# A decoder step on one Trainium2 core: the last pass of two projections taken token tile by token tile

## The chip, the core and the metric

The kernel runs on one core of one Trainium2 chip. It is timed in device microseconds from launch to end, without profiling. Its engines are TensorE (PE: matmuls and transposes), VectorE (DVE), ScalarE (ACT), GpSimd (POOL) and SyncE (SP), which only issues DMAs here. Each engine runs its own list of instructions in order, and the lists wait for each other by semaphores that are written by hand.

## The reference, cut to what matters

One layer over 512 prompt tokens and 64 sample tokens (8 requests of 8), model width D = 1024, all in float32:

```python
def rms_norm(x, g):
    y = x32 * lax.rsqrt(jnp.mean(x32 * x32, axis=-1, keepdims=True) + EPS)
    return (y * g.astype(jnp.float32)).astype(x.dtype)
...
    h = rms_norm(x, ln1_pre_l) * (1 + sc1) + sh1
    mixed, new_state = mix_fn(h @ w_in_l)          # pooling heads and sparse attention
    x = x + g1 * rms_norm(mixed @ w_out_l, ln1_post_l)
    h = rms_norm(x, ln2_pre_l) * (1 + sc2) + sh2
    f = jnp.square(jax.nn.relu(h @ w_ff1_l)) @ w_ff2_l        # 1024 -> 4096 -> 1024
    x = x + g2 * rms_norm(f, ln2_post_l)
```

A norm over a row needs the sum of squares of all 1024 columns, so nothing of a token's output can be scaled before its last column is there.

## The kernel before, in words

**Token tiles.** Tokens lie on partitions: four prompt tiles of 128 (t = 0 to 3) and one tile with the 64 sample tokens (t = NT = 4), whose high and low parts are stacked on 128 partitions and added later. A projection's output of 512 columns is one PSUM bank, and tile t uses bank 3 + t, both for columns 0 to 511 (nh = 0) and for 512 to 1023 (nh = 1).

**Split weights.** Each float32 matmul is three matmuls of a high and a low part (two for the sample tile). A piece of weights (1 MB) is loaded by SP into `raw`, ACT writes its high part to `w_split` (L1168), DVE the low part (L486), and the semaphore `lo_ready` releases it to PE. `raw` and `w_split` have two slots each. The order of pieces is the list `PIECES`: `wo` 0 to 3 are the output projection (two halves of the contraction for nh = 0, then two for nh = 1), `w1` and `w2` the MLP in four quarters.

**Projections.** `by_token` (L948) takes one column half: the first piece over all tiles (0, 1, 2, 3, NT), then the second piece over all tiles; each tile's bank is full only in the second. ACT copies a full bank to `out_t`; for the sample tile ACT copies the low rows to `half_s` and DVE adds them (`sum_rows`, L1844; in the MLP L1907 and L1908).

**Between the two projections (called the middle below).** For each tile after nh = 1: ACT squares 1024 columns with a running sum (L1204), DVE turns the sum into a mean (L1558), ACT takes the root, DVE the reciprocal (L1565), DVE multiplies by it and the gate (`gated`, L1834), POOL adds the residual in `x_res` (L697), then square, mean, root and reciprocal again and DVE scales to `out_t` (`normalise`, L1570), two tiles behind (LAG = 2). PE then transposes (`turned_hidden`, L740): it waits until all five tiles are normalised (L779). ACT and DVE scale, shift and split the transposed rows while PE goes on, and the first MLP matmul follows.

**The end.** In the last quarter of the MLP with nh = 1 DVE adds each bank to `out_t` (L1897) as it gets full, and one tile behind does `last_residual` (L1837): gate, then residual (L1841). POOL stores 1024 columns of each tile (L705, L707), waits for the stores, and the program ends for all engines together (the trace puts the engines' last instructions on L269).

Of the kernel before, what the change touches and what calls it, by code (L numbers as in the profile page):

```python
# [21 lines left out]
D = 1024  # L22
# [23 lines left out]
LAG = 2  # L46
EARLY = 4
QF = 4
# [105 lines left out]
def plan_norms():  # L154


    order = [(0, t) for t in range(NT + 1)]
    for j in range(NT + 1 + LAG):
        order += [(1, j)] * (j <= NT) + [(2, j - LAG)] * (j >= LAG)
    order += [(3, t) for t in range(NT + 1)]  # L160
    return {key: n for n, key in enumerate(order)}


NORM = plan_norms()
# [102 lines left out]
def build_program(nc, a, o, spans):  # L267
    ctx = ExitStack()
    with ctx:  # L269
# [24 lines left out]
        ss = sb("ss", [128, 4 * (NT + 1)])  # L294
        rstd = sb("rstd", [128, 4 * (NT + 1)])
# [85 lines left out]
        halves_mlp = sb("halves_mlp", [128, 512], stack=mlp)  # L381
        mlp.close()
# [113 lines left out]
        def _(sp):  # L496
# [79 lines left out]
            for n in range(AT[("wo", 0)] + 2, len(PIECES)):  # L576
                load_piece(n)

        @block.gpsimd
        def _(pool):  # L580
# [121 lines left out]
            for t in range(NT + 1):  # L702
                pool.wait_ge(S["y_ok"], t + 1)
                if t < NT:
                    pool.dma_start(yp[:, t, :], x_res[:, t, :]).then_inc(S["y_out"], 16)  # L705
                else:
                    pool.dma_start(o["y_s"].rearrange("b t d -> (b t) d"), x_res[0:TS, t, :]).then_inc(S["y_out"], 16)  # L707
            pool.wait_ge(S["y_out"], 16 * (NT + 1))
# [6 lines left out]
        def _(pe):  # L715
# [431 lines left out]
            for nh in range(2):  # L1147
                by_token("wo", 2 * nh, ("wo", nh), act_hi, act_lo, act_s)
# [4 lines left out]
            for f in range(QF):  # L1153
# [4 lines left out]
                for nh in range(2):  # L1158
                    by_token("w2", 4 * f + 2 * nh, ("w2", f, nh), hid_hi, hid_lo, hid_s, f)
# [22 lines left out]
        def _(act):  # L1182
# [14 lines left out]
            def square(k, t, src):  # L1197

                r = rows_of(t)
                if NORM[k, t]:  # L1200
                    act.wait_ge(S["squares"], NORM[k, t])
                junk = stage[:, :, :].rearrange("p a n -> p (a n)")
                x = (NT + 1) * k + t
                run(junk[0:r, :], src[0:r, t, :], ACT.Square, accum_out=ss[0:r, x:x + 1]).then_inc(S["squares"], 1)  # L1204

            def root(k, t):
                x = (NT + 1) * k + t
                act.wait_ge(S["mean_ok"], NORM[k, t] + 1)
                run(rstd[0:rows_of(t), x:x + 1], ss[0:rows_of(t), x:x + 1], ACT.Sqrt).then_inc(S["root_ok"], 1)
# [17 lines left out]
            act.wait_ge(S["pad_zero2"], 1)  # L1227
            out = full(act, "cT")
# [12 lines left out]
            for t in range(NT + 1):  # L1241
                square(0, t, x_in)
# [233 lines left out]
            keep_tokens("wo", (), 0, True, 0, AT[("wo", 1)])  # L1476
            hi_until(AT[("wo", 2)] + 3)

            for j in range(NT + 1 + LAG):
                if j < NT:  # L1480
                    free(run(out_t[:, j, 512:D], full(act, ("wo", 1, j))[:, :]), ("wo", 1, j))
                elif j == NT:
                    out = full(act, ("wo", 1, NT))
                    evacuated(act, ("wo", 0, NT))
                    run(half_s[:, :], out[TS:2 * TS, :]).then_inc(S["low_rows"], 1)
                if j <= NT:
                    evacuated(act, ("wo", 1, j))
                    square(1, j, out_t)
                if j >= LAG:
                    act.wait_ge(S["residual"], j - LAG + 1)  # L1490
                    square(2, j - LAG, x_res)
                if j <= NT:
                    root(1, j)
                if j >= LAG:
                    root(2, j - LAG)
# [29 lines left out]
            for t in range(NT):  # L1525
                evacuated(act, ("w2", QF - 1, 1, t))
                square(3, t, out_t)
                root(3, t)
            keep_tokens("w2", (QF - 1,), 1, False, 1 + 2 * QF, 0)
            evacuated(act, ("w2", QF - 1, 1, NT))  # L1530
            square(3, NT, out_t)
            root(3, NT)

        @block.vector
        def _(dve):
# [18 lines left out]

            def mean(k, t):
                x, r = (NT + 1) * k + t, rows_of(t)
                dve.wait_ge(S["squares"], NORM[k, t] + 1)
                nc.vector.tensor_scalar(ss[0:r, x:x + 1], ss[0:r, x:x + 1], 1.0 / D, EPS, ALU.mult, ALU.add)\  # L1558
                    .then_inc(S["mean_ok"], 1)
# [379 lines left out]
```

## Time and profile before

| | us |
|---|---|
| median of three runs | 976.88 (974.75 to 990.48) |
| profiled execution, its own time | 972.49 |
| its span, first to last instruction | 970.8 |
| PE busy in the span | 861.6 (89%) |
| last matmul of the output projection to the first transpose | 488.9 to 509.0 |
| first to last matmul of the MLP | 517.6 to 949.9 |

The span is 1.69 us shorter than the time of the same execution. All times of the trace count from the start of the span. Each line of the page's parts names the source line, the engine, the operation, and output and inputs by the program's names; `bank` is PSUM.

### The profile page before, as it was taken

The page shows a single profiled execution, that of the slowest core. Times are in us where ns is not written, and L with a number is a line of the kernel's source. Part 1 is how long each engine was busy: PE and PEld are TensorE (multiplying, and loading weights), DVE is VectorE, ACT ScalarE, POOL GpSimd, SP SyncE. Part 2 cuts the span into 40 slices and gives each one's busy share as a digit, 9 for nine tenths or more (in the row PEclk, how much of TensorE's full clock was granted, in tenths as well). Part 3 has the DMA queues.
Part 4 walks back from the last instruction along what each step waited for, and adds up shares of the span by engine and source line. Part 5 has one row for each costly group of instructions (what it writes and reads, how often), then busy time and mean ns, then how long its engine had stood idle before and what let it go on. Part 6 is the DMA issues. An engine that isn't in the chain of part 4 may idle for free.

```text
span 970.8 us, 11293 instructions
## 1 busy us (share of the span) xinstructions
PE 861.6 (89%) x4136; PEld 646.7 (67%) x4136; DVE 453.4 (47%) x859; ACT 335.3 (35%) x615; POOL 97.9 (10%) x145
## 2 busy tenths in 40 slices
PE   2798899999978968879919999999999999999991
PEld 0486448877735545438816888888888888888880
DVE  0342899768466962311385441134334333343335
ACT  3453632242454742211447242233212331233121
POOL 2141210007032310000040000000000000000000
PEclk9889799999978997999969999999999999999996
DMA  9741300412385766654201212222122222222102
GB/s 327 261 126 51 95 11 2 129 52 66 122 271 185 246 211 202 195 174 163 86 22 44 87 54 77 87 87 87 59 72 87 87 87 70 67 82 86 44 1 98
DMA packets 68122, 105.83 MB, mean 109 GB/s; under 512 B 6906, under 2 KB 32134, under 8 KB 68058
## 3 DMA queue, kind: packets, MB, share of 16 engines
q1 hardware_dynamic: 62882, 94.12, 30.3%
q0 software_dynamic: 3952, 8.75, 2.7%
q10 hardware_dynamic: 1232, 2.23, 0.6%
q8 instruction: 33, 0.54, 0.2%
q14 instruction: 23, 0.19, 0.1%
HBM read 100.04 MB, written 5.15 MB: 108 GB/s over the span
## 4 chain that ended last, share of the span: by engine, by line
PE 70%; DVE 8%; issue 4%; ACT 3%; SPq 2%; DMA 1%; POOL 1%; ACTq 0%; DVEq 0%; POOLq 0%
PE bank L737 68%; PE bank L740 3%; DVE out_t L1834 1%; DVE score L1645 1%; ACT stage L1193 1%; DVE probs L1740 1%; SPq L535 1%; DVE keys L1547 1%; SPq L553 1%; ACT probs L1193 1%; DVE out_t L1570 1%; DMA raw<-in_ada_w 1%; DVE act_lo L1547 1%; DVE x_res L1841 1%; DMA pages<-in_cache_k 0%
## 5 line engine op out<-in xcount | busy, mean ns | idle before, releaser
L737 PE MATMUL bank<-act_hi,w_split 128*128 128x512 f32 (+1 forms) x800 | 259.9, 398 | 0.0
L486 DVE TENSOR_TENSOR w_split<-raw,w_split 128x2048 fp32r<-128x2048 f32 (+2 forms) x48 | 107.3, 2238 | 155.7 <-ACT w_split L1168 155.6
L737 PEld LDWEIGHTS bank<-act_hi,w_split 128*128 128x128 f32 (+1 forms) x800 | 151.7, 190 | 33.8 <-issue 1.0
L737 PE MATMUL bank<-w_split,hid_hi 128*128 128x512 f32 x512 | 161.2, 396 | 0.0
L737 PE MATMUL bank<-act_lo,w_split 128*128 128x512 f32 (+1 forms) x400 | 157.6, 394 | 0.0
L1168 ACT ACTIVATE w_split<-raw 128x2048 fp32r<-128x2048 f32 (+2 forms) x48 | 89.3, 1862 | 106.4 <-PE bank L737 106.4
L737 PEld LDWEIGHTS bank<-w_split,hid_hi 128*128 128x128 f32 x512 | 95.9, 188 | 22.9
L737 PE MATMUL bank<-w_split,hid_lo 128*128 128x512 f32 x256 | 101.3, 396 | 0.0
L737 PEld LDWEIGHTS bank<-act_lo,w_split 128*128 128x128 f32 (+1 forms) x400 | 76.0, 190 | 15.9
L737 PE MATMUL bank<-w_split,act_s 128*128 128x512 f32 (+1 forms) x248 | 60.6, 386 | 0.0
L737 PE MATMUL bank<-w_split,act_hi 128*128 128x512 f32 x192 | 59.6, 392 | 0.0
L737 PEld LDWEIGHTS bank<-w_split,hid_lo 128*128 128x128 f32 x256 | 48.1, 188 | 11.6
L1193 ACT ACTIVATE stage<-bank 128x512 f32<-128x512 f32 (+3 forms) x43 | 25.3, 587 | 83.9 <-PE bank L737 80.9
L1874 DVE TENSOR_TENSOR stage<-stage 128x512 f32<-128x512 f32 x32 | 22.2, 693 | 67.8 <-ACT stage L1193 66.2
L737 PEld LDWEIGHTS bank<-w_split,act_s 128*128 128x128 f32 x248 | 46.1, 188 | 9.4
L705 POOL DMA_DIRECT2D out_y_p<-x_res x4 | 2.1, 538 | 447.8 <-DVE x_res L1841 447.8
L737 PEld LDWEIGHTS bank<-w_split,act_hi 128*128 128x128 f32 x192 | 35.7, 188 | 8.0 <-issue 0.8
L737 PE MATMUL bank<-w_split,act_lo 128*128 128x512 f32 x96 | 37.4, 390 | 0.0
L1897 DVE TENSOR_TENSOR out_t<-bank,out_t 128x512 f32<-128x512 f32 x24 | 16.5, 689 | 36.1 <-PE bank L737 36.1
L737 PE MATMUL bank<-raw,c_pad 128*32 128x512 f32 x160 | 28.5, 794 | 5.0 <-DMA raw<-in_ada_w 5.0
L740 PE MATMUL bank<-cst,pages 128*128 128x128 f32 (+2 forms) x168 | 26.0, 303 | 7.6 <-DMA pages<-in_cache_k 5.8
L737 PE MATMUL bank<-w_split,hid_s 128*128 128x512 f32 x128 | 32.5, 396 | 0.0
(240 smaller groups left out, 1120.0 us busy)
## 6 DMA issues: line engine op xcount, KB each, us to landing
raw<-in_w_ff SPq DMA_DIRECT2D x32, 1024.0 KB, 5.3
raw<-in_ada_w SPq DMA_DIRECT2D x20, 1024.0 KB, 5.4
raw<-in_w_in SPq DMA_DIRECT2D x10, 1024.0 KB, 5.3
pages<-in_cache_k SPq DMA_DIRECT2D x32, 256.0 KB, 2.9
v_pages<-in_cache_v SPq DMA_DIRECT2D x32, 256.0 KB, 3.0
pages<-in_ada_w SPq DMA_DIRECT2D x4, 1024.0 KB, 12.5
raw<-in_w_out SPq DMA_DIRECT2D x4, 1024.0 KB, 6.6
x_in<-in_x_prompt SPq DMA_DIRECT2D x1, 2048.0 KB, 14.5
```

Source lines behind the costliest of these rows:

```text
L486: return ops.tensor_tensor(lo, r, hi.bitcast(F32), ALU.subtract)
L535: return sp.value_load(table[0:1, i:i + 1], min_val=0, max_val=ck.shape[0] - 1)
L553: sp.dma_start(slots[:, b % 2, g, :], cache[bass.ds(page_of(b * NPG + g), 1)].rearrange("o p n -> (o p) n"))\
L737: return nc.tensor.matmul(out, lhsT, rhs, start=start, stop=stop, skip_group_check=True)
L740: return nc.tensor.transpose(out, in_, cc("ident")[0:k, 0:k])
L1168: return nc.scalar.activation(hi, r, ACT.Copy)
L1193: return nc.scalar.activation(out, in_, func, **kw)
L1547: return nc.vector.tensor_tensor(out, x, hi.bitcast(F32), ALU.subtract)
L1570: nc.vector.tensor_scalar(dst[0:r, t, :], src[0:r, t, :], rstd_of(k, t), None, ALU.mult)\
L1645: ins = nc.vector.scalar_tensor_tensor(score[t][:, 0:L], r, wi[:, t, h:h + 1], score[t][:, 0:L], ALU.mult, ALU.add)
L1874: nc.vector.tensor_tensor(stage[:, n % 2, :], stage[:, n % 2, :], stage[:, n % 2, :], ALU.mult)\
L1897: free(nc.vector.tensor_tensor(out_t[:, t, s], full(dve, ("w2", f, nh, t))[:, :], out_t[:, t, s], ALU.add), ("w2", f, nh, t))
```

## The change

**PE.** A new function `by_token_late` takes the second column half of the output projection and of the last MLP quarter in another order: the sample tile and tile 0 over the first piece, both over the second piece, then tile 1 over both pieces, then tile 2, then tile 3. It uses both pieces of weights from near its start, and starts with the bank of the sample tile.

**Norms.** The left half's squares are summed ahead of the right half, in `ss_left`; one DVE instruction makes their means, which ACT's root takes as its bias (scale 1/D). No mean per tile is left, in the input's norm neither. In the middle ACT squares banks directly and DVE multiplies banks by the gate into `out_t`, so no copy of a bank is left. The residual is one DVE instruction (product with the reciprocal, plus `x_res`) and no longer POOL's. The tiles come in the order NT, 0, 1, 2, 3, one behind.

**Other places.** The low part of the first `w1` piece is made by POOL, and its high part by ACT between two tiles. The outputs are stored by SP in column halves, ten stores of 256 KB or less instead of POOL's five.

```diff
 TAKEN = -3.0e38
 NRAW, NSPLIT = 2, 2
...
+            yp = o["y_p"][0].rearrange("(t p) d -> p t d", p=128)
+            ys = o["y_s"].rearrange("b t d -> (b t) d")
+            for j, t in enumerate(LATE):
+                for nh in range(2):
+                    s = slice(512 * nh, 512 * nh + 512)
+                    sp.wait_ge(S["y_ok"], 2 * j + nh + 1)
+                    if t < NT:
+                        sp.dma_start(yp[:, t, s], x_res[:, t, s]).then_inc(S["y_out"], 16)
+                    else:
+                        sp.dma_start(ys[:, s], x_res[0:TS, t, s]).then_inc(S["y_out"], 16)
+            sp.wait_ge(S["y_out"], 16 * 2 * (NT + 1))
...
-            for t in range(NT + 1):
-                r = rows_of(t)
-                pool.wait_ge(S["gated"], t + 1)
-                if t == 0:
-                    pool.wait_ge(S["x_again"], 32)
-                nc.gpsimd.tensor_tensor(x_res[0:r, t, :], x_res[0:r, t, :], out_t[0:r, t, :], ALU.add)\
-                    .then_inc(S["residual"], 1)
...
-            yp = o["y_p"][0].rearrange("(t p) d -> p t d", p=128)
...
-            pool.wait_ge(S["y_out"], 16 * (NT + 1))
+            pool.wait_ge(S["half_done"], 3)
+            split_lo(pool, nc.gpsimd, AT[("w1", 0)]).then_inc(lo_ready, 1)
...
+            def by_token_late(kind, first, name, x_hi, x_lo, x_s):
+
+                outs = {}
+                for tiles in ((NT, 0), (1,), (2,), (3,)):
+                    for half in range(2):
+                        hi, lo, _ = piece(kind, first + half)
+                        for t in tiles:
+                            if half == 0:
+                                outs[t] = claim(name + (t,))
+                            for k4 in range(4):
+                                k = 4 * half + k4
+                                if t < NT:
+                                    tok = slice(128 * t, 128 * t + 128)
+                                    mm(outs[t][:, :], x_hi[:, k, tok], hi[:, k4, :], k == 0, False)
+                                    mm(outs[t][:, :], x_hi[:, k, tok], lo[:, k4, :], False, False)
+                                    last = mm(outs[t][:, :], x_lo[:, k, tok], hi[:, k4, :], False, k == 7)
+                                else:
+                                    mm(outs[t][:, :], x_s[:, k, :], hi[:, k4, :], k == 0, False)
+                                    last = mm(outs[t][:, :], x_s[:, k, :], lo[:, k4, :], False, k == 7)
+                            if half == 1:
+                                done(last, name + (t,))
+                        if half == 0 and tiles == (3,):
+                            last.then_inc(S["half_done"], 1)
...
-            for nh in range(2):
-                by_token("wo", 2 * nh, ("wo", nh), act_hi, act_lo, act_s)
+            by_token("wo", 0, ("wo", 0), act_hi, act_lo, act_s)
+            by_token_late("wo", 2, ("wo", 1), act_hi, act_lo, act_s)
...
-            keep_tokens("wo", (), 0, True, 0, AT[("wo", 1)])
-            hi_until(AT[("wo", 2)] + 3)
...
-                    free(run(out_t[:, j, 512:D], full(act, ("wo", 1, j))[:, :]), ("wo", 1, j))
...
+            for t in range(NT):
+                square((1, t, 0), full(act, ("wo", 0, t))[:, :], left_sum(1, t))
+            keep_tokens("wo", (), 0, False, 0, AT[("wo", 1)])
+            evacuated(act, ("wo", 0, NT))
+            square((1, NT, 0), out_t[0:TS, NT, 0:512], left_sum(1, NT))
...
+            for j in range(NT + 2):
                 if j <= NT:
-                    evacuated(act, ("wo", 1, j))
...
+                    t = LATE[j]
+                    if j == NT:
+                        hi_until(AT[("wo", 2)] + 3)
+                    out = full(act, ("wo", 1, t))
+                    if t == NT:
+                        run(half_s[:, :], out[TS:2 * TS, :]).then_inc(S["low_rows"], 1)
+                        evacuated(act, ("wo", 1, NT))
+                        square((1, NT, 1), out_t[0:TS, NT, 512:D], sum_of(1, NT))
+                    else:
+                        square((1, t, 1), out[:, :], sum_of(1, t))
+                    root(1, t)
+                if j:
+                    t = LATE[j - 1]
+                    act.wait_ge(S["residual"], j)
+                    square((2, t), x_res[0:rows_of(t), t, :], sum_of(2, t))
+                    root(2, t)
```

DVE's side of the same places, the middle and the end:

```diff
+            def residual(k, t, y, s):
 
                 r = rows_of(t)
-                gate = gate_p if t < NT else gate_s
-                nc.vector.scalar_tensor_tensor(out_t[0:r, t, :], out_t[0:r, t, :], rstd_of(k, t),
-                                               gate[0:r, :], ALU.mult, ALU.mult).then_inc(S["gated"], 1)
...
-                dve.wait_ge(S["gated"], NT + 2 + t)
-                r = rows_of(t)
-                nc.vector.tensor_tensor(x_res[0:r, t, :], x_res[0:r, t, :], out_t[0:r, t, :], ALU.add)\
-                    .then_inc(S["y_ok"], 1)
+                x = (NT + 1) * k + t
+                return nc.vector.scalar_tensor_tensor(x_res[0:r, t, s], y, rstd[0:r, x:x + 1], x_res[0:r, t, s],
+                                                      ALU.mult, ALU.add)
...
+            for j in range(NT + 2):
                 if j <= NT:
-                    mean(1, j)
-                if j >= LAG:
-                    mean(2, j - LAG)
-                if j <= NT:
-                    gated(1, j)
-                if j >= LAG:
-                    normalise(2, j - LAG, out_t, x_res)
+                    t = LATE[j]
+                    if t == NT:
+                        sum_rows(1)
+                        link(gate_rows(1, 1))
+                    else:
+                        dve.wait_ge(S["squares"], SQUARE[1, t, 1] + 1)
+                        ins = nc.vector.tensor_tensor(out_t[:, t, 512:D], full(dve, ("wo", 1, t))[:, :], gate_p[:, 512:D], ALU.mult)
+                        free(ins, ("wo", 1, t))
+                        evacuated(dve, ("wo", 1, t))
+                    rstd_of(1, t)
+                    residual(1, t, out_t[0:rows_of(t), t, :], slice(0, D)).then_inc(S["residual"], 1)
+                if j:
+                    normalise(2, LATE[j - 1], out_t, x_res)
...
+            for j, t in enumerate(LATE):
+                r = rows_of(t)
+                y, g = out_t[0:r, t, right], gated_right[0:r, j % 2, :]
+                if t == NT:
+                    dve.wait_ge(S["low_rows"], 3 + 2 * f + 1)
+                    link(nc.vector.tensor_tensor(y, y, half_s[:, :], ALU.add))
+                free(nc.vector.tensor_tensor(y, full(dve, ("w2", f, 1, t))[0:r, :], y, ALU.add), ("w2", f, 1, t))
+                evacuated(dve, ("w2", f, 1, t))
+                link(nc.vector.tensor_tensor(g, y, (gate_p if t < NT else gate_s)[0:r, right], ALU.mult))
+                rstd_of(3, t)
+                residual(3, t, out_t[0:r, t, 0:512], slice(0, 512)).then_inc(S["y_ok"], 1)
+                residual(3, t, g, right).then_inc(S["y_ok"], 1)
```

The lists of instructions before and after show the places that the prediction speaks of. Each row has the line, the operation, the tiles and what it waits for.

**PE where the column halves of the output projection meet.** `bank7` is the sample tile's, `bank3` tile 0's. Before:

```order
L737 MATMUL bank7<-w_split,act_s 128x512 x8
L737 MATMUL bank3<-w_split,act_hi 128x512 [waits bank_free3,lo_ready]
L737 MATMUL bank3<-w_split,act_hi 128x512
L737 MATMUL bank3<-w_split,act_lo 128x512
L737 MATMUL bank3<-w_split,act_hi 128x512 x2
L737 MATMUL bank3<-w_split,act_lo 128x512
```

With the change:

```order
L745 MATMUL bank7<-w_split,act_s 128x512 [waits bank_free7,lo_ready]
L745 MATMUL bank7<-w_split,act_s 128x512 x7
L745 MATMUL bank3<-w_split,act_hi 128x512 [waits bank_free3]
L745 MATMUL bank3<-w_split,act_hi 128x512
L745 MATMUL bank3<-w_split,act_lo 128x512
L745 MATMUL bank3<-w_split,act_hi 128x512 x2
L745 MATMUL bank3<-w_split,act_lo 128x512
L745 MATMUL bank3<-w_split,act_hi 128x512 x2
L745 MATMUL bank3<-w_split,act_lo 128x512
L745 MATMUL bank3<-w_split,act_hi 128x512 x2
L745 MATMUL bank3<-w_split,act_lo 128x512
L745 MATMUL bank7<-w_split,act_s 128x512 [waits lo_ready]
```

The first matmul of the right half now waits for bank 7, which the last matmuls of the left half have just filled, instead of bank 3; and the second piece (the wait for `lo_ready` alone) comes after two tiles instead of five.

**DVE before the transposes**, from the last tile's sum on. Before:

```order
L1565 RECIPROCAL rstd<-rstd 64x1 [waits root_ok]
L1834 SCALAR_TENSOR_TENSOR out_t<-out_t,rstd,gate_s 64x1024 [waits dve_chain]
L1565 RECIPROCAL rstd<-rstd 128x1 [waits root_ok]
L1570 TENSOR_SCALAR out_t<-x_res,rstd 128x1024 [waits dve_chain]
L1558 TENSOR_SCALAR ss<-ss 128x1 [waits squares]
L1565 RECIPROCAL rstd<-rstd 128x1 [waits root_ok]
L1570 TENSOR_SCALAR out_t<-x_res,rstd 128x1024 [waits dve_chain]
L1558 TENSOR_SCALAR ss<-ss 64x1 [waits squares]
L1565 RECIPROCAL rstd<-rstd 64x1 [waits root_ok]
L1570 TENSOR_SCALAR out_t<-x_res,rstd 64x1024 [waits dve_chain]
```

With the change, from tile 3's bank on:

```order
L1922 TENSOR_TENSOR out_t<-bank6,gate_p 128x512 [waits bank_full6,squares]
L1616 RECIPROCAL rstd<-rstd 128x1 [waits root_ok,bank_free6]
L1890 SCALAR_TENSOR_TENSOR x_res<-out_t,rstd,x_res 128x1024 [waits dve_chain]
L1616 RECIPROCAL rstd<-rstd 128x1 [waits root_ok]
L1621 TENSOR_SCALAR out_t<-x_res,rstd 128x1024 [waits dve_chain]
L1616 RECIPROCAL rstd<-rstd 128x1 [waits root_ok]
L1621 TENSOR_SCALAR out_t<-x_res,rstd 128x1024 [waits dve_chain]
```

The gate of a half tile reads a bank, the residual is DVE's, and after tile 3's residual two tiles are still to be normalised.

**ACT at the same place**, with the change:

```order
L1228 ACTIVATE stage,ss<-x_res 128x1024 [waits squares,residual]
L1228 ACTIVATE rstd<-ss,eps 128x1 [waits squares]
L1203 ACTIVATE w_split<-raw 128x8x256 [waits half_done,raw_landed0]
L1228 ACTIVATE stage,ss<-bank6 128x512 [waits squares,bank_full6]
L1228 ACTIVATE rstd<-ss,mean_left 128x1 [waits squares,half_mean]
L1228 ACTIVATE stage,ss<-x_res 128x1024 [waits squares,residual]
L1228 ACTIVATE rstd<-ss,eps 128x1 [waits squares]
```

The high part of the first `w1` piece stands ahead of tile 3's squares, and waits until PE has done with the first piece (`half_done`).

**POOL and SP at the end of their lists.** Before, POOL:

```order
L697 TENSOR_TENSOR x_res<-x_res,out_t 128x1024 [waits x_again,gated]
L697 TENSOR_TENSOR x_res<-x_res,out_t 128x1024 [waits gated] x3
L697 TENSOR_TENSOR x_res<-x_res,out_t 64x1024 [waits gated]
L700 DMA ln_post<-in_ln2_post 128x1024 [waits bank_free7]
L705 DMA out_y_p<-x_res 128x1024 [waits y_ok] x4
L707 DMA out_y_s<-x_res 64x1024 [waits y_ok]
L269 UNCONDITIONAL_BRANCH [waits stage_out0,outs,stage_out1,y_out]
```

With the change, POOL:

```order
L711 DMA x_res<-in_x_prompt 128x4x1024
L712 DMA x_res<-in_x_sample 64x1024
L714 DMA ln_post<-in_ln2_post 128x1024 [waits bank_free7]
L496 TENSOR_TENSOR w_split<-raw,w_split 128x8x256 [waits hi_ready,half_done]
L275 UNCONDITIONAL_BRANCH [waits outs,stage_out0,stage_out1]
```

With the change, SP:

```order
L537 DMA raw<-in_w_ff1 128x8x256 [waits lo_ready] x4
L540 DMA raw<-in_w_ff2 128x4x512 [waits lo_ready] x4
L597 DMA out_y_s<-x_res 64x512 [waits y_ok] x2
L595 DMA out_y_p<-x_res 128x512 [waits y_ok] x8
L275 UNCONDITIONAL_BRANCH [waits y_out]
```

POOL's five additions and its five stores are gone, it makes one low part, and nothing of its list comes later; the stores stand at the end of SP's list.

## Rows read from the trace of the kernel before

**Rows 1.** the page, part 4: the chain that ended last, shares by engine

```profile
PE 70%; DVE 8%; issue 4%; ACT 3%; SPq 2%; DMA 1%; POOL 1%; ACTq 0%; DVEq 0%; POOLq 0%
```

**Rows 2.** windows from:to; us, PE busy (matmuls), PEclk, DMA share, GB/s

```profile
489.00:509.00 20.00, 0.00 (x0) 0.63 0.08 25
494.50:495.00 0.50, 0.00 (x0) 0.50 0.00 0
518.00:560.00 42.00, 42.00 (x184) 1.00 0.23 75
```

**Rows 3.** timeline of PE: start us, us, engine, line, operation, names, forms

```profile
461.56 1.98 PE L737 MATMUL bank<-w_split,act_s 128*128 128x512 f32 x8
463.37 0.61 PE L737 MATMUL bank<-w_split,act_hi 128*128 128x512 f32 x2
...
486.94 1.98 PE L737 MATMUL bank<-w_split,act_s 128*128 128x512 f32 x8
509.00 4.53 PE L740 MATMUL bank<-cst,out_t 128*128 128x128 f32 x20 [20.08 <-DVE out_t L1570]
...
517.58 0.50 PE L737 MATMUL bank<-act_hi,w_split 128*128 128x512 f32 x1
```

**Rows 4.** timelines of ACT and DVE where the column halves meet

```profile
463.57 0.59 ACT L1193 ACTIVATE half_s<-bank 64x512 f32<-64x512 f32 x1 [1.22 <-PE bank L737]
464.07 1.90 ACT L1168 ACTIVATE w_split<-raw 128x2048 fp32r<-128x2048 f32 x1
...
464.20 0.69 DVE L1847 TENSOR_TENSOR out_t<-bank,half_s 64x512 f32<-64x512 f32 x1 [8.92 <-ACT half_s L1193]
466.00 2.29 DVE L486 TENSOR_TENSOR w_split<-raw,w_split 128x2048 fp32r<-128x2048 f32 x1 [1.12 <-ACT w_split L1168]
```

**Rows 5.** timelines of ACT and DVE between output projection and transposes

```profile
479.61 1.06 ACT L1193 ACTIVATE stage<-out_t 128x1024 f32<-128x1024 f32 x1
...
482.07 0.20 ACT L1193 ACTIVATE rstd<-ss 128x1 f32<-128x1 f32 x1
...
482.51 1.28 DVE L1834 SCALAR_TENSOR_TENSOR out_t<-out_t,rstd,gate_p 128x1024 f32<-128x1024 f32 x1
...
484.60 2.77 DVE L1834 SCALAR_TENSOR_TENSOR out_t<-out_t,rstd,gate_p 128x1024 f32<-128x1024 f32 x1
...
491.01 2.86 DVE L1570 TENSOR_SCALAR out_t<-x_res,rstd 128x1024 f32<-128x1024 f32 x1
...
506.75 0.75 DVE L1570 TENSOR_SCALAR out_t<-x_res,rstd 128x1024 f32<-128x1024 f32 x1
```

**Rows 6.** timelines of DVE and POOL, two places where both work at once

```profile
331.67 0.69 DVE L1547 TENSOR_TENSOR keys<-bank,turned_hi 128x512 fp32r<-128x512 f32 x1
...
331.82 0.73 POOL L668 TENSOR_TENSOR near<-toep,score 128x256 f32<-128x256 f32 x1 [1.79 <-DVE small L1743]
...
483.88 2.40 POOL L697 TENSOR_TENSOR x_res<-x_res,out_t 128x1024 f32<-128x1024 f32 x1 [46.41 <-DVE out_t L1834]
```

**Rows 7.** timelines of ACT, DVE and PE at the end

```profile
923.77 0.59 ACT L1193 ACTIVATE half_s<-bank 64x512 f32<-64x512 f32 x1 [11.09 <-PE bank L737]
...
925.12 0.68 DVE L1908 TENSOR_TENSOR out_t<-bank,out_t 64x512 f32<-64x512 f32 x1
...
959.93 1.22 DVE L1841 TENSOR_TENSOR x_res<-x_res,out_t 64x1024 f32<-64x1024 f32 x1
...
947.84 2.03 PE L737 MATMUL bank<-w_split,hid_s 128*128 128x512 f32 x8
```

**Rows 8.** the last line: sequencer, operation, ns min/median/max, first and last start

```profile
L269 SPq DRAIN  x1: 123/123/123, 901.4 to 901.4; - x1
...
L269 POOLq DRAIN  x1: 6118/6118/6118, 964.5 to 964.5; - x1
```

**Rows 9.** DMA issues: names, queue, times, KB, median us from issue to landing

```profile
out_k_p<-stage ACTq DMA_DIRECT2D x4, 256.0 KB, 2.2
...
out_y_s<-x_res POOLq DMA_DIRECT2D x1, 256.0 KB, 2.8
```

More of the change, by code:

```diff
@@ L45 @@
 NRAW, NSPLIT = 2, 2
-LAG = 2
+LATE = (NT, *range(NT))
 EARLY = 4
@@ L154, in plan_norms @@
 def plan_norms():
[L157 to L164, printed above, removed]
+    squares = [(0, t) for t in range(NT + 1)] + [(1, t, 0) for t in range(NT + 1)]
+    roots = [(0, t) for t in range(NT + 1)]
+    for j in range(NT + 2):
+        if j <= NT:
+            squares.append((1, LATE[j], 1))
+            roots.append((1, LATE[j]))
+        if j:
+            squares.append((2, LATE[j - 1]))
+            roots.append((2, LATE[j - 1]))
+    squares += [(3, t, 0) for t in range(NT + 1)] + [(3, t, 1) for t in LATE]
+    roots += [(3, t) for t in LATE]
+    return {key: n for n, key in enumerate(squares)}, {key: n for n, key in enumerate(roots)}
+SQUARE, ROOT = plan_norms()
 def plan_banks():
@@ L294, in build_program @@
         ss = sb("ss", [128, 4 * (NT + 1)])
+        ss_left = sb("ss_left", [128, 2 * (NT + 1)])
+        mean_left = sb("mean_left", [128, 2 * (NT + 1)])
+        eps = sb("eps", [128, 1])
         rstd = sb("rstd", [128, 4 * (NT + 1)])
@@ L1241, in _ @@
             for t in range(NT + 1):
-                square(0, t, x_in)
+                square((0, t), x_in[0:rows_of(t), t, :], sum_of(0, t))
             modulation(3)
@@ L1475, in _ @@
             hi_until(AT[("wo", 0)] + 3)
[L1476 to L1495 removed]
+            for t in range(NT):
[4 more added lines that the diff above has]
+            for j in range(NT + 2):
+                if j <= NT:
+                    t = LATE[j]
[6 more added lines that the diff above has]
+                        square((1, NT, 1), out_t[0:TS, NT, 512:D], sum_of(1, NT))
+                    else:
+                        square((1, t, 1), out[:, :], sum_of(1, t))
[5 more added lines that the diff above has]
+                    root(2, t)
             turned_hidden(1)
@@ L1524, in _ @@
             act.wait_ge(S["w1_done"], 2 * DFF // 256)
-            for t in range(NT):
+            for t in range(NT + 1):
+                evacuated(act, ("w2", QF - 1, 0, t))
+                square((3, t, 0), out_t[0:rows_of(t), t, 0:512], left_sum(3, t))
+            for t in LATE:
+                if t == NT:
+                    keep_tokens("w2", (QF - 1,), 1, False, 1 + 2 * QF, 0)
                 evacuated(act, ("w2", QF - 1, 1, t))
-                square(3, t, out_t)
+                square((3, t, 1), out_t[0:rows_of(t), t, 512:D], sum_of(3, t))
                 root(3, t)
[L1529 to L1532, printed above, removed]
         @block.vector
@@ L1571, in normalise @@
                     .then_inc(S["normed"], 1)
-            for t in range(NT + 1):
-                mean(0, t)
             for t in range(NT + 1):
@@ L1912, in _ @@
                     lo_until(AT[("w2", 4 * f + 2 * nh + 1)] + 3)
-            mean(3, NT)
-            last_residual(NT)
+            for t in range(NT):
+                dve.wait_ge(S["squares"], SQUARE[3, t, 0] + 1)
+                nc.vector.tensor_tensor(out_t[:, t, 0:512], out_t[:, t, 0:512], gate_p[:, 0:512], ALU.mult)
+            gate_rows(3, 0)
+            left_means(3)
+            f, right = QF - 1, slice(512, D)
+            for j, t in enumerate(LATE):
+                r = rows_of(t)
+                y, g = out_t[0:r, t, right], gated_right[0:r, j % 2, :]
+                if t == NT:
+                    dve.wait_ge(S["low_rows"], 3 + 2 * f + 1)
[6 more added lines that the diff above has]
+                residual(3, t, g, right).then_inc(S["y_ok"], 1)
 _OUTS = [("y_p", (1, TP, D)), ("y_s", (DB, DS, D)),
```

89 lines of the change are left out of this document (50 added, 39 removed).

## The prediction, made before the changed kernel was run

> **What bounds the kernel now.** I read the page first: in the chain of work that ended last, PE has 70% of the span (970.8 us) and DVE 8% [rows 1]. No matmul is added or removed, so only stretches in which PE waits can give something back. The windows show where: from 489 to 509 PE does no matmul at all, and from 518 on it is busy throughout [rows 2]. The timeline of PE gives the edges: the output projection's last matmuls start at 486.94 and take 1.8 us to the end of the stage, at 488.75 (they last 1.81 when others follow, 461.56 to 463.37); the first transpose starts at 509.00, and the first MLP matmul at 517.58 [rows 3]. So the middle costs 20.2 us of waiting and 8.6 us of transposing. The second stretch is the end: the last matmul ends at 949.9 [rows 7] and the span at 970.8, which is 20.9 us. Both are chains of ACT and DVE instructions, tile after tile, and the second has something more: the last residual ends at 961.15 [rows 7], the sample tile's store takes 2.8 us [rows 9], and then POOL's sequencer is in a DRAIN of 6.12 us from 964.5 on, after which all engines end. SP's DRAIN took 0.12 us [rows 8].
>
> **PE's order, middle.** A tile's twelve matmuls over one piece take 2.72 us: 463.37 to 486.94 is eight of them and one sample group of 1.81 [rows 3]. The change keeps their sum, but its first group needs bank 7. That bank is full at 463.57, ACT copies the low rows in 0.59, and DVE's addition ends at 464.89 [rows 4]. PE goes on at 464.95 instead of 463.37, **+1.6 us**. The second piece is wanted at 464.95 + 1.81 + 2.72 = 469.5, and its low part is ready at 468.3 [rows 4]: no second wait. Tile 0's bank is then complete near 474.1, tile 1's near 479.5, tile 2's near 484.9, tile 3's at 490.4. A reader sees it full 0.2 us later, as at 463.57 against 463.37: 490.6.
>
> Each tile has 5.4 us of matmuls above it, and wants from DVE 0.69 (gate), 1.28 (residual), 0.75 (scale) and from ACT two squares; root and reciprocal take 0.44 from the root's start to the instruction that wants them, 482.07 to 482.51 [rows 4, 5]. That is some 3.1 us on DVE and 2.3 on ACT. Both fit, so tiles NT, 0 and 1 are done before tile 3's bank is full, and only tile 3 and the scaling of tile 2 remain. The left half's five squares and five gates cost nothing for the same reason; without that cover they would be some 7 us. The input norm loses five instructions on 128 x 1, of which PE's first matmuls on weights wait for none: nothing, and under 1 us if it were otherwise.
>
> **After tile 3's bank.** ACT squares 512 columns of a bank: no row has that, the bounds are 0.59 for a copy of such a bank [rows 4] and 1.06 for a square of 1024 [rows 5]; I take 0.72, near the copy, since the width decides. That gives 491.3. The gate reads the bank and takes 0.69: 492.0. The root (0.20) runs beside it, the reciprocal follows: 492.2. The residual takes 1.28 if nothing holds it: 493.5.
>
> Something may hold it. POOL makes the low part of the first `w1` piece: PE has done with `w_split`'s slot at 484.9 + 2.7 = 487.65, ACT's high part takes 1.9 (to 489.8) [rows 4], and POOL begins. Its price has no row for 2048 columns: 2.40 us for 1024 and 0.73 for 256 [rows 6] make 4.6 by the slope and 5.8 by eight of the small ones; DVE's 2.29 for the same job [rows 4] is the lower bound. I take 4.7, nearest to the row of 1024, so POOL is busy until 494.5. In the trace, DVE's product of two SBUF tensors started at 484.60 and took 2.77 instead of 1.28 while POOL's addition ran from 483.88 to 486.28; it ended 1.09 after POOL. The scaling at 491.01 took 2.86 instead of 0.75 beside the next addition [rows 5, 6]. So the residual ends at 494.5 + 1.1 = 495.6, not 493.5: **2.1 us** lost to POOL. A DVE subtraction with one input in PSUM took its usual 0.69 with POOL at work beside it, but it had started first [rows 6]; I let the gate pass. The Trainium skill (SBUF — State Buffer, "SBUF: two separate sides") has it so: the port pair of DVE and GpSimd is locked for a whole instruction, against DVE instructions with two SBUF inputs or in a two-port mode. Were the gate held too, it would add 0.7 us.
>
> Then ACT squares tile 3's residual (1.06, and 0.1 that I add for reading the sum): 496.8; root and reciprocal 0.44: 497.2; scaling 0.75: 498.0. Tile 2's scaling lies beside the square. PE starts to transpose at 498.0 instead of 509.0: **middle −11.0 us** (−13.1 with POOL out of the way, −9.9 with POOL at 5.8). Transposes and the shift stay at 8.6 us. Before, the clock granted to PE was at its lower level, 0.50 of full (1.2 GHz), when it had been idle [rows 2]; with less idle time it may be higher for the first transposes, for which I count nothing.
>
> **The end.** In the last quarter the same wait for bank 7 is longer, since DVE has two additions: ACT's copy starts at 923.77, the second addition ends at 925.80 [rows 7], and PE goes on at 925.85 instead of 923.57: **+2.3 us**. The last bank (tile 3's) is full at 949.9 + 2.3 = 952.2. Addition 0.69, square 0.72, root and reciprocal 0.44: 954.05; the gate lies beside the square. Two residuals of 512 columns, 0.64 (half of 1.28) to 0.69 each: 955.4. Then SP stores 128 x 512: 2.2 us in a row of the same size from ACT's queue, 2.8 from POOL's [rows 9]; I take 2.4 with the other half still in flight, 957.9. SP's DRAIN and the meeting of the engines, 0.4: 958.3. The other eight stores land under later tiles. Before, the span ended at 970.8: **end −12.5 us**, of which 6.1 is POOL's DRAIN, now 450 us early in a list with nothing behind it, and 5.7 the shorter work after the last residual's counterpart (961.15 to 955.4).
>
> **The sum.** −11.0 − 12.5 = −23.5 us. Against the profiled execution's own time of 972.49 that is 949.0, 2.4% less. The median of the three runs, 976.88, lies 0.45% above that execution, and 23.5 off it gives **953**, which I forecast.
>
> **The rivals.**
> *The DRAIN stays.* For: its row shows only that it stood last [rows 8], and it may be the cost of ending whatever was issued, on SP too with ten stores. Against: SP's, behind all the loads, took 0.12 [rows 8]. Then the gain is 17.4 and the time 959.5, within 2%. The Trainium skill (VectorE: DVE Perf Modes, "The DRAIN you can't avoid") gives such closing DRAINs some 12 ns on each engine; by that the 6.12 us are no cost of POOL's queue and would go nowhere. The row speaks against the page: 6118 ns. Chance 0.09.
> *POOL's low part is slow.* It writes fp32r over a piece cut in eight chunks, which no POOL row does. At twice my price (9.4 us) tile 3's residual waits until 500.3, everything behind by 4.7 us: 958. Chance 0.07.
> *Slower: the clock.* Both late passes now begin after a PE wait (1.6 and 2.3 us). If PE were granted its lower level after them and held there, the 25.4 and 26.3 us of matmuls behind them would take twice as long: up to +51.7, a time of 1005. Against 23.5 us of gain it decides from about 23.5 us of full-speed matmul work done at the lower level, nearly a whole pass. For: the level did drop in the long idle stretch [rows 2]. Against: that was after PE had been idle, and the MLP ran at 1.00 right after [rows 2]. A drop for a few us costs 2 to 5 and stays on the faster side of even. Chance of slower than before by over 2%: 0.03; of a small loss that leaves the time at 957 to 960: 0.04.
> *The change gives no earlier start*, because some wait still ties the tiles: only if DVE or ACT falls more than 5.4 us behind per tile, of which the lists show no sign. Middle 0, end −12.5: 964. Chance 0.03.
>
> **Numbers.** My case keeps 0.74 and reaches from 948 (POOL out of the way, stores at 2.2, and runs nearer to the profiled execution) to 957 (POOL at 5.8, the gate held, 1 us more at the end, scatter of the runs). With the two rivals at 958 to 960 the range is **947 to 961**. What can be told from no change is about 2%, here 957.3. Faster by over 2%: 0.74 and a part of the rivals, 0.76; within 2%: 0.21; slower: 0.03.
>
> **What would show it.** The first transpose about 7.5 us after the output projection's last matmul, not 20; two PE gaps of 1.6 and 2.3 us where the column halves meet; one DVE residual near 3.4 us beside POOL's low part, the other four at 1.28; POOL's DRAIN in mid-program; the span's end some 6 us after the last matmul. Wrong would be: a long DRAIN at the end on any engine, PE gaps within the late passes, or a granted clock under 1.00 in them.

## The result, and the profile after

| us | before | changed |
|---|---|---|
| median | 976.66 (974.75 to 990.48, 4 runs) | 948.89 (945.28 to 952.71, 4 runs) |
| ratio, 95% interval | | 0.9734 (0.9679 to 0.9788) |
| profiled execution, and its span | 972.49, 970.8 | 945.28, 943.4 |

The change makes the kernel 2.7% faster; forecast were 953 and a range of 947 to 961. The profiled executions lie 27.2 us apart, where the sum had 23.5. Some executions fall into a slower state (990.48 us is one); the ratios here leave them out and the medians keep them, so the two can differ by some 0.2%.

In the chain that ended last (the page's part 4) the share of DVE has halved against [rows 1]:

```profile
PE 72%; DVE 4%; ACT 2%; issue 2%; DMA 1%; SPq 1%; POOL 0%; DVEq 0%; ACTq 0%
```

The chain in the middle, from 480 to 520 us (start us, us, what). It is the counterpart of the 20.08 us in [rows 3]:

```profile
479.98 10.67 PE bank L745 x47
...
490.67 0.70 ACT stage L1228 x2
...
491.39 0.70 DVE out_t L1922
...
492.12 0.17 DVE rstd L1616
...
492.31 3.38 DVE x_res L1890
...
495.71 1.16 ACT stage L1228 x2
...
496.89 0.30 ACT rstd L1228
...
497.42 0.77 DVE out_t L1621
...
498.23 1.13 PE bank L748 x4
...
506.88 13.35 PE bank L745 x57
```

PE's last matmul ends at 490.63 and the first transpose starts at 498.23: 7.6 us, of which the one residual at L1890 is 3.4. The timelines of POOL, DVE and PE, for the place where the column halves meet (the first row) and for the middle:

```profile
464.96 0.47 PE L745 MATMUL bank<-w_split,act_s 128*128 128x512 f32 x1 [1.49 <-DVE out_t L1896]
...
486.88 1.28 DVE L1890 SCALAR_TENSOR_TENSOR x_res<-out_t,rstd,x_res 128x1024 f32<-128x1024 f32 x1
...
490.09 4.50 POOL L496 TENSOR_TENSOR w_split<-raw,w_split 128x2048 fp32r<-128x2048 f32 x1 [46.33 <-ACT w_split L1203]
...
491.39 0.69 DVE L1922 TENSOR_TENSOR out_t<-bank,gate_p 128x512 f32<-128x512 f32 x1 [2.37 <-ACT stage L1228]
...
492.31 3.37 DVE L1890 SCALAR_TENSOR_TENSOR x_res<-out_t,rstd,x_res 128x1024 f32<-128x1024 f32 x1
```

The residual takes 1.28 us when POOL is idle and 3.37 when POOL works until 494.59. The gate, with one input in PSUM, starts in the midst of POOL's work and takes its usual 0.69.

The end, as the chain has it:

```profile
909.25 0.60 ACT half_s L1228
...
909.88 0.69 DVE out_t L1967
...
910.60 0.69 DVE out_t L1968
...
911.42 25.91 PE bank L745 x112
...
937.35 0.70 DVE out_t L1986
...
938.08 0.73 ACT stage L1228 x2
...
939.49 0.75 DVE x_res L1890
```

and the last line's rows by sequencer (columns as in [rows 8]):

```profile
L275 POOLq DRAIN  x1: 10008/10008/10008, 490.3 to 490.3; - x1
...
L275 SPq DRAIN  x1: 7/7/7, 943.2 to 943.2; - x1
```

PE pauses from 909.22 to 911.42 for bank 7, its last matmul ends at 937.32, and the span ends at 943.4. POOL's DRAIN lies in mid-program. It is longer than before, but until 494.59 POOL's own L496 was still at work beside it; 5.7 of its 10.0 us come after that.

Cut at three points, the two spans compare so (us):

| stretch | before | changed | difference |
|---|---|---|---|
| from PE's pause of 2.94 us ahead of the output projection (begins at 421.5 in both) to its last matmul | 67.4 | 69.2 | +1.8 |
| no matmul, until the first transpose | 20.1 | 7.6 | −12.5 |
| first transpose to last matmul | 440.9 | 439.1 | −1.8 |
| behind the last matmul | 20.9 | 6.1 | −14.8 |

In the third stretch the new pause of 2.2 us is contained, so the rest of it became 4.0 us shorter. That was not in my sum.

### The profile page after: what moved, and what is told of

The parts are those of the page before. It is cut to its first block, busy times and chain, and to the rows that moved or that the text cites. A ratio compares the mean times of both kernels' runs of the same rounds, so it can differ in the third digit from the quotient of the medians.

```text
span 943.4 us, 11350 instructions
## 1 busy us (share of the span) xinstructions
PE 855.5 (91%) x4136; PEld 645.3 (68%) x4136; DVE 449.0 (48%) x862; ACT 335.5 (36%) x627; POOL 88.1 (9%) x136
## 4 chain that ended last, share of the span: by engine, by line
PE 72%; DVE 4%; ACT 2%; issue 2%; DMA 1%; SPq 1%; POOL 0%; DVEq 0%; ACTq 0%
PE bank L745 69%; PE bank L748 3%; DVE probs L1789 1%; ACT stage L1228 1%; DMA raw<-in_ada_w 1%; DVE keys L1602 1%; SPq L545 1%; SPq L563 0%; DVE x_res L1890 0%; DVE act_lo L1602 0%; DMA pages<-in_cache_k 0%; POOL near L689 0%; DMA out_k_p<-stage 0%; ACT pv_rows L1228 0%; DVE probs L1804 0%
## 5 line engine op out<-in xcount | busy, mean ns | idle before, releaser
L496 DVE TENSOR_TENSOR w_split<-raw,w_split 128x2048 fp32r<-128x2048 f32 (+2 forms) x47 | 105.0, 2236 | 143.0 <-ACT w_split L1203 142.9
L745 PE MATMUL bank<-w_split,hid_hi 128*128 128x512 f32 x512 | 159.2, 392 | 0.0
L1228 ACT ACTIVATE stage<-bank 128x512 f32<-128x512 f32 (+3 forms) x51 | 30.1, 591 | 95.5 <-PE bank L745 92.2
L1228 ACT ACTIVATE probs<-probs,small 128x128 f32<-128x128 f32 (+4 forms) x36 | 20.9, 580 | 31.6 <-DVE small L1792 25.7
L1228 ACT ACTIVATE stage_s<-bank 128x128 f32<-128x128 f32 (+1 forms) x24 | 9.2, 385 | 63.8 <-PE bank L745 63.8
## 6 DMA issues: line engine op xcount, KB each, us to landing
pages<-in_ada_w SPq DMA_DIRECT2D x4, 1024.0 KB, 12.5
x_in<-in_x_prompt SPq DMA_DIRECT2D x1, 2048.0 KB, 14.6
```

Source lines behind the costliest of these rows:

```text
L496: return ops.tensor_tensor(lo, r, hi.bitcast(F32), ALU.subtract)
L745: return nc.tensor.matmul(out, lhsT, rhs, start=start, stop=stop, skip_group_check=True)
L1228: return nc.scalar.activation(out, in_, func, **kw)
```

## The experiments

Four questions: do the two waits that I priced cost what I said, is the DRAIN a matter of who stores last, does the chain or PE's order bring the gain, and where do the 4.0 us come from? Stretches below are cut as in the table above, each from one profiled execution. What goes before them differs by up to 9 us among the 13 profiles (that pause began between 417.9 and 426.8), though before and changed agree there. So differences of 2 us are read from stretches and not from medians. The kernels were also timed on different occasions, each with before beside it: the changed kernel, e1 to e4, e5 to e8, and e9 to e11, where before had 976.7, 976.1, 976.3 and 973.2. Medians are compared within one of these, and the ratio to before across them.

**The two waits.** `e1_after_again` is the changed kernel unaltered.

> The changed kernel once more, unaltered, as the yardstick for the three kernels beside it. Both theories of the extra gain (about 4 us in the second MLP projection's steady matmuls) speak here. If it is of the program (where its tiles lie), the step between matmuls of the second MLP projection is 228.9 ns again, and the time 945 to 950 us. If it was chance of one execution, the step comes out anywhere between 228.9 and 233.3 ns.

Measured: 948.56 us (5 runs), ratio to before 0.9759 (0.9740 to 0.9779); stretches 69.1, 7.6, 439.1, 6.1. The step between matmuls of the second MLP projection is 228.9 ns again (what it means comes with the 4.0 us below).

```diff
 # e2_low_on_dve: POOL
-            pool.wait_ge(S["half_done"], 3)
-            split_lo(pool, nc.gpsimd, AT[("w1", 0)]).then_inc(lo_ready, 1)
 # DVE, behind the last normalise
-            dve.wait_ge(lo_ready, NTH[AT[("w1", 0)]] + 1)
-            split[0] = AT[("w1", 0)] + 1
+            lo_until(AT[("w1", 0)] + 1)
 # e3_tile0_first: by_token_late; e4_both has the two edits
-                for tiles in ((NT, 0), (1,), (2,), (3,)):
+                for tiles in ((0, NT), (1,), (2,), (3,)):
```

> The low part of the first piece of w1 is made by VectorE after the last normalise, and no longer by GpSimd beside the last residual. My theory, that GpSimd's 4.50 us operation holds VectorE's residual back: the residual takes 1.28 us in place of 3.37, the transposes before the MLP start 2.1 us earlier (496.1), and the time is about 2.1 us shorter. The rival, that the residual is long for its reads from PSUM: it stays near 3.4 us, and the time is the same or up to 2.3 us longer, as VectorE has the low part to make in the transposes' way.

The timeline of DVE and PE:

```profile
497.77 1.28 DVE L1888 SCALAR_TENSOR_TENSOR x_res<-out_t,rstd,x_res 128x1024 f32<-128x1024 f32 x1
...
501.46 2.28 DVE L496 TENSOR_TENSOR w_split<-raw,w_split 128x2048 fp32r<-128x2048 f32 x1
501.61 1.75 PE L746 MATMUL bank<-cst,out_t 128*128 128x128 f32 x7 [5.52 <-DVE out_t L1619]
```

The residual is at 1.28 and the stretch without matmuls at 5.5 instead of 7.6: the theory holds for the wait. The whole did not show it, with 948.64 us against 948.56 (ratios 0.9748 and 0.9759). In the profiled execution the third stretch is 440.7 instead of 439.1, and the granted clock accounts for that. Its windows (from:to, us, busy of PE, PEld, DVE, ACT, POOL, PEclk, DMA share, GB/s) around the pause at 912.6:

```profile
904.00:912.00 8.00, 8.00 (x37) 6.57 (x36) 2.79 (x5) 0.00 (x0) 0.00 (x0) 1.00 0.00 0
912.00:920.00 8.00, 5.79 (x19) 4.28 (x18) 6.31 (x8) 5.90 (x12) 0.00 (x0) 0.79 0.00 0
```

The missing 0.21 of 8 us is 1.7 us; the changed kernel's own profile had 1.00 behind the same pause.

> In the last pass of both projections the first group is tile 0 and the small tile in that order, and no longer the small tile first, so that bank 7 (which ScalarE must empty first) is asked for one accumulation group later. My theory, that TensorE's pause of 1.5 and 2.2 us at the column-half meeting is the wait for that bank: both pauses go but for some 0.3 us, and the time is about 3 us shorter (1.3 in the middle, 2 at the end). The rival, that TensorE there waits for the weights' low half or for the first token tile's operands: the pause stays and the time is the same within 0.5 us.

Measured: 945.16 us, ratio to before 0.9716 (0.9666 to 0.9766), 3.4 us below e1 by the medians, though the intervals of the two ratios overlap. Both pauses are gone; PE's timeline shows 0.28 us left in the middle and, at the end, matmuls that follow each other where 2.21 us stood (0.23 us are left further on, at 916):

```profile
468.58 0.74 PE L745 MATMUL bank<-w_split,act_hi 128*128 128x512 f32 x2 [0.28 <-DVE w_split L496]
...
909.31 1.99 PE L745 MATMUL bank<-w_split,hid_s 128*128 128x512 f32 x8
911.14 0.62 PE L745 MATMUL bank<-w_split,hid_hi 128*128 128x512 f32 x2
```

So the wait was bank 7's. In its profile the third stretch is 440.1 where some 436.9 was due without the pause; the clock was granted at 0.88, 0.55 and 0.60 from 500 to 512, whereas the changed kernel had 1.00 from 505 on:

```profile
504.00:508.00 4.00, 3.33 (x16) 2.64 (x16) 2.08 (x3) 3.90 (x8) 0.00 (x0) 0.55 0.00 0
508.00:512.00 4.00, 4.00 (x13) 3.10 (x12) 2.67 (x4) 1.89 (x4) 0.00 (x0) 0.60 0.00 0
```

> The low part on VectorE and tile 0 first, together. If the two waits lie one behind the other on the path, the gains add: about 5 us shorter than the changed kernel. If one hides the other, it is no more than the larger of the two, 3 us.

Measured: 945.28 us, 0.9701 (0.9659 to 0.9742); the stretch without matmuls 5.5 again, no pauses, and again a late dip of the clock (0.50 and 0.81 from 508 to 516). The two waits go together, so neither hides the other. The time does not follow: the four stretches are 69.3, 5.5, 440.2 and 6.0, together 521.0 against the changed kernel's 522.0, since 3.3 us of the third went to the dip and 1.3 of the first to an earlier one, and the median is e3's. That the gains add in time is not shown.

The dips need none of the edits. e6 below has the changed kernel's instructions up to its stores, pauses included, and its profile has both: one behind the middle and one behind the pause of 2.2 us. Its third stretch is 443.8 instead of 439.1. The windows:

```profile
508.00:512.00 4.00, 4.00 (x12) 3.14 (x11) 2.56 (x5) 1.88 (x4) 0.00 (x0) 0.57 0.00 0
...
912.00:920.00 8.00, 6.54 (x22) 5.25 (x23) 6.66 (x9) 5.18 (x11) 0.00 (x0) 0.79 0.00 0
```

**The DRAIN.**

```diff
 # e5_before_sp_stores: before, on POOL (and the same five stores behind SP's loads)
-                pool.wait_ge(S["y_ok"], t + 1)
-                    pool.dma_start(yp[:, t, :], x_res[:, t, :]).then_inc(S["y_out"], 16)
 # e6_after_pool_stores: changed, ten stores
-                    sp.wait_ge(S["y_ok"], 2 * j + nh + 1)
+                    pool.wait_ge(S["y_ok"], 2 * j + nh + 1)
```

> The kernel before, with its stores of y issued by SyncE's queue and no longer by GpSimd's; nothing else. My theory, that GpSimd's DRAIN of 6.1 us comes last only because GpSimd issues the last stores: the DRAIN moves to the middle of the program, and the time is 6 to 7 us shorter than before (6.1, and some 0.8 of issue and landing). The rival, that the DRAIN stands at the end of any program in which GpSimd has issued DMAs: it stays there, and the gain is at most 1 us.

Measured: 969.63 us against 976.3, 0.9918 (0.9875 to 0.9962); the last stretch 14.6 instead of 20.9.

> The changed kernel, with its stores of y (in column halves as they are) issued by GpSimd again. My theory: a DRAIN of about 6 us (or up to 10, since it was 10.0 us in mid-program) stands behind the last store, and the time is 6 to 7 us longer than the changed kernel's, up to 11 if the longer DRAIN comes. The rival, that the end became shorter by the column halves alone: about 1 us longer.

Measured: 955.41 us, 0.9765 of before (0.9684 to 0.9846); the last stretch 13.3 instead of 6.1. The ratio lies only 0.1 to 0.3% above those of the changed kernel (0.9734, and 0.9759 in e1), with an interval of 0.8% to either side, so it does not resolve the 6 to 7 us; the stretch does. POOL's row in e5, and in e6:

```profile
L269 POOLq DRAIN  x1: 8624/8624/8624, 503.1 to 503.1; - x1
```

```profile
L275 POOLq DRAIN  x1: 6527/6527/6527, 947.5 to 947.5; - x1
```

The rivals that the DRAIN stays, or that column halves alone shorten the end, are out: it stands where POOL's own list ends, in both kernels. In e6 it is 6.5 of the 7.2 us; the landing is 0.4 of the rest (2.5 us from POOL's queue, 2.1 from SP's). Whether POOL would have so long a DRAIN without having issued any DMA was not tried.

**Chain or order.**

```diff
 # e8_old_order: changed kernel
-LATE = (NT, *range(NT))
+LATE = (*range(NT), NT)
-            by_token_late("wo", 2, ("wo", 1), act_hi, act_lo, act_s)
+            by_token("wo", 2, ("wo", 1), act_hi, act_lo, act_s)
 # and the same for the last quarter of w2
```

> The changed kernel's norm chain in column halves, its gate, residual and stores, but TensorE's order of the last passes as before (small tile last, both column halves of a token tile not brought together by the new grouping). My theory, that the gain comes from the shorter chain behind the last bank and from the end of the program, not from the order: the transposes before the MLP start near 500 us, the end loses the 2.3 us wait for bank 7 and has a somewhat longer tail, and the time is within 2 us of the changed kernel's. The rival, that the order is what pays: at least 10 us longer than the changed kernel.

Measured: 957.43 us, 0.9794 of before (0.9715 to 0.9872). By the ratios that is 3 to 6 us above the changed kernel (0.9759 and 0.9734), with the same wide interval. The profiled executions lie 9.4 apart, of which 4.3 lie ahead of the stretches. The stretches are 67.4, 12.2, 436.7 and 10.8: 5.1 us more in all than the changed kernel's. Both theories are wrong: mine allowed 2 us, the rival wanted 10. DVE's timeline of the last additions shows what I had left out:

```profile
931.96 0.69 DVE L1986 TENSOR_TENSOR out_t<-bank,out_t 128x512 f32<-128x512 f32 x1 [7.76 <-PE bank L745]
...
935.43 0.68 DVE L1986 TENSOR_TENSOR out_t<-bank,out_t 128x512 f32<-128x512 f32 x1
...
938.89 0.68 DVE L1986 TENSOR_TENSOR out_t<-bank,out_t 128x512 f32<-128x512 f32 x1
...
942.35 0.68 DVE L1986 TENSOR_TENSOR out_t<-bank,out_t 128x512 f32<-128x512 f32 x1
...
946.52 0.68 DVE L1986 TENSOR_TENSOR out_t<-bank,out_t 64x512 f32<-64x512 f32 x1
```

A tile costs the chain 3.46 us (935.43 to 938.89). In the old order a token tile's bank is full 12 matmuls behind the last one, 12 x 0.229 = 2.75 us, so the tiles queue and the end is late by what has piled up, and by the sample tile. In the new order 24 matmuls, 5.5 us, lie between, and each tile is done before the next bank is full.

**The 4.0 us.** I compared the distance between starts of neighbouring matmuls, in the stretches where PE never waits and the clock is 1.00. In the second MLP projection it was 233.3 ns before and 228.9 after; in the first one it was 227 in both. These passes have 8 x 112 = 896 matmuls, and 896 x 4.4 ns = 3.9 us of the 4.0. Up to the last pass nothing in PE's instructions there has changed, but the new small tiles push `hid_hi` and all SBUF tiles behind it 160 bytes further.

```diff
 # e7_before_padded: before; e9, e10, e11: e4 with 64, 32 and 96 bytes
+        sb("pad", [128, 40])
         rstd = sb("rstd", [128, 4 * (NT + 1)])
```

> The kernel before, with an unused tile of 160 bytes per partition ahead of the small tiles, so that the hidden activations' tile hid_hi starts at the address that it has in the changed kernel (125216 in place of 125056); no instruction is changed. If the matmul's step in the second MLP projection hangs on that address, it falls from 233.3 to 228.9 ns and the time by about 4 us. The rival, that it varies from run to run or hangs on the order of the work: no change within 1 us.

Measured: 970.29 us against 976.3, 0.9944 (0.9900 to 0.9988); distance 228.9 ns; third stretch 436.7 instead of 440.9. An unused tile alone makes the kernel faster by the missing term. PE's rows of before, and of e7, in each case with 45 matmuls from the first start to the second (10.50 us, and 10.30):

```profile
936.64 0.63 PE L737 MATMUL bank<-w_split,hid_hi 128*128 128x512 f32 x2
...
947.14 0.63 PE L737 MATMUL bank<-w_split,hid_hi 128*128 128x512 f32 x2
```

```profile
931.17 0.62 PE L738 MATMUL bank<-w_split,hid_hi 128*128 128x512 f32 x2
...
941.47 0.62 PE L738 MATMUL bank<-w_split,hid_hi 128*128 128x512 f32 x2
```

> The kernel with the low part on VectorE and tile 0 first, and an unused tile of 64 bytes per partition ahead of the reciprocal roots' tile; hid_hi and all tiles behind it lie 64 bytes further (125280 in place of 125216). The steps seen so far: 233.3 ns with hid_hi at 125056 (a multiple of 128), 228.9 ns at 125216 (a multiple of 128, and 32), and 226.9 ns in the first MLP projection, whose operands lie at a multiple of 128, and 96. If the step goes by the place within 128 bytes, it is 226.9 ns here and the time about 2 us shorter than that kernel's 945.3; if it goes by the place within 64 bytes, it stays at 228.9 and the time at 945.

> The same with a tile of 32 bytes; hid_hi lies at 125248, a multiple of 64. If the place within 64 bytes decides, the step in the second MLP projection is 233.3 ns again and the time about 4 us longer (949); if the place within 128 bytes decides, the step is some other one than 233.3 and 228.9.

> The same with a tile of 96 bytes; hid_hi lies at 125312, a multiple of 128 again. By either rule of the address the step is 233.3 ns and the time about 949 us. If it stays at 228.9, neither rule holds, and the 160 bytes did it in another way.

| `hid_hi` at, past a multiple of 128 bytes | kernels | distance, ns | time, us, and ratio to before |
|---|---|---|---|
| 0 | before, e11 | 233.3 | 948.14, 0.9738 (e11, 2 runs) |
| 32 | changed, e7, e4 | 228.9 | 945.28, 0.9701 (e4, 4 runs) |
| 64 | e10 | 233.3 | 944.84, 0.9704 (2 runs) |
| 96 | e9 | 226.7 | 943.30, 0.9691 (6 runs) |

The second MLP projection by groups (matmuls, busy, mean ns of one, which includes an end that overlaps the next), from 580 to 600 us, of e9 and e11:

```profile
L744 PE MATMUL bank<-w_split,hid_hi 128*128 128x512 f32 x50 | 15.4, 389 | 0.0
```

```profile
L744 PE MATMUL bank<-w_split,hid_hi 128*128 128x512 f32 x53 | 16.7, 395 | 0.0
```

At these places, the one within 64 bytes decides most, and the one within 128 bytes some more (228.9 or 226.7). In the profiles of e9 and e11 the clock is back at 1.00 before the MLP's matmuls, and their third stretches are 435.5 and 441.3: 5.8 us apart, where 896 x 6.6 ns make 5.9. e10 came back to 233.3 as the first rule has it. Its time did not rise by the 4 us expected, and two runs don't resolve them; its third stretch is 443.9, with the clock at 0.57 from 500 to 508. e9 has the lowest median of all, 0.9691 of before (0.9663 to 0.9718), but its interval overlaps that of e4, so that it is faster than e4 is shown by the distance alone.

## Why the prediction was right

- **The meeting of the column halves.** Predicted +1.6 and +2.3 us; 1.49 and 2.21 in the trace, and e3 shows both to be bank 7's: with tile 0 ahead of the sample tile neither is needed.
- **The middle.** Predicted: the residual blocked by POOL's low part and 2.1 us late, transposes at 498.0, −11.0. Measured: 3.37 us, 498.23, −10.8. POOL's price of 4.7, from two smaller shapes by the slope, was 4.50. e2 confirms the mechanism: without POOL beside it the residual takes 1.28. The Trainium skill (SBUF — State Buffer, "SBUF: two separate sides") has a port pair locked for a whole instruction against DVE operations with two SBUF inputs; by that rule the gate from PSUM passes, and the trace agrees (0.69 beside POOL).
- **The end.** Predicted 958.3 for the span, −12.5. With the pause set against it the last stretch gave −12.6: DRAIN 6.1 by [rows 8] (6.3 by e5), the rest the chain.
- **The DRAIN.** It moved to 490.3 and is hidden, as forecast. The rival that it stays, at 0.09, is refuted by e5 and e6.
- **The clock.** The rival that the late passes run at the lower level did not come; but a part of it did in e2 and e6, where 1.7 us went behind the pause of 2.2. It belongs to what I had called "a drop for a few us", whose lower end (2) it misses slightly. In the changed kernel's own profile the clock was at 0.50, its lower level, from 494 to beyond 502, but had come back by 505, before the MLP's matmuls.
- **What the sum lacked.** "From one profiled execution's time, −23.5": the foreseen terms gave −23.4, and the other 4.0 came from the matmuls of the second MLP projection, by the address of their operands (e7). That is also why the median is 949 where I had 953. The order of instructions could not show it, and I had counted PE's unchanged work at nothing.
- **What I took for one cause were two.** I priced the chain as if each tile were done before the next bank. That holds in the new order, which the prediction was about, but not in the old one, and so my expectation for e8 failed. Undoing the order (e8) gives back 5.1 us, though it saves both pauses. By stretches, from kernel to kernel: the DRAIN brings 6.3 us (20.9 to 14.6, e5); the chain's new form, its store halves included, 7.8 in the middle (20.1 to 12.2) and 3.8 at the end (14.6 to 10.8, e8); the address 4.2 (440.9 to 436.7); the order 2.8 in the middle and 2.3 at the end, net of its pauses. Together that is 27.2, beside 27.4 between the spans; since each step starts from the stretches of the one before, the total agrees by itself, and another sequence could share it out differently. The 7.8 also hold what else changed in the middle between e5 and e8, as the residual's move from POOL to DVE.

Open is which operand's address decides: hid_hi, hid_lo, hid_s and what lies behind were moved together in every padded kernel. Open is also why the granted clock falls soon after a pause in some executions and stays at 1.00 in others.

## What to carry to other kernels

A serial chain behind the last accumulation is worth more than its length if banks come faster than the chain serves them: compare the distance of banks (2.75 or 5.5 us here) with the chain per tile (3.46). Let the engine whose sequencer closes quickly issue the last stores, and see that a long instruction of POOL does not lie beside the one residual that is waited for. When a kernel moves by more or less than the sum of its waits, compare the start-to-start distance of the untouched matmuls first; a new small tile can shift the operands of others. And before a median is read against another kernel's, look at the granted clock of both profiles in the stretch that the edit touches.

## What was not expected of the hardware

- The same matmul (128 x 128 on 512 columns of fp32r, clock at 1.00) came every 233.3, 228.9, 233.3 or 226.7 ns as its operands' tiles lay 0, 32, 64 or 96 bytes past a multiple of 128. Over 896 matmuls that is up to 5.9 us.
- POOL's closing DRAIN took 6.1 and 6.5 us at the end of the program and 8.6 and 10.0 in its middle, where it began beside POOL's own last instructions and ended 6.1 and 5.7 us after them; SP's, with up to ten stores ahead of it, took 7 ns.
- The granted clock soon after PE has resumed differs between executions of the same instructions: from 504 to 512 it was 1.00 in e1 and 0.58 and 0.57 in e6, and from 912 to 920 it was 1.00 and 0.79. In the profiled executions of e2, e3 and e4 1.7, 3.2 and 3.3 us went that way behind the middle or the later pause, of 2.1, 3.2 and 5.3 us of waits that the edits had removed.
